# Gating of the second attention moved a stage later, weight sums on GpSimd, and three weight loads issued later

## The reference

```python
def _merge(a_att, b_att, a_z, b_z, g_a, g_b, w_o_a, w_o_b, w_out):
    o_a = (a_att * jax.nn.silu(a_z)) @ w_o_a
    o_b = (b_att * jax.nn.silu(b_z)) @ w_o_b
    merged = jax.nn.sigmoid(g_a) * o_a + jax.nn.sigmoid(g_b) * o_b
    return merged @ w_out
```

```python
    kv = x @ kv_w                       # keys and values
    q = (x @ w_q).reshape(...)          # queries
```

## Time and profile before

| | us |
|---|---|
| median of 3 runs (lowest, highest) | 3465.53 (3465.18, 3466.58) |
| the profiled execution | 3466.58 |
| its span | 3464.7 |
| matrix engine busy in the span | 3048.4 (88%) |
| VectorE busy | 1214.3 (35%) |
| ScalarE busy | 844.5 (24%) |
| GpSimd busy | 413.3 (12%) |

### The profile page before, as it was taken

One profiled execution on the slowest core, in us unless ns is written; L12 is line 12 of the kernel. 1 busy time (PEld: TensorE's weight loads), 2 busy tenths in 40 slices (PEclk: granted clock), 3 DMA queues, 4 the chain that ended last, 5 costly groups with the idle time before them and its releaser, 6 DMA issues. The chain is left out here.

```text
span 3464.7 us, 41966 instructions
## 1 busy us (share of the span) xinstructions
PE 3048.4 (88%) x16815; PEld 1726.1 (50%) x16815; DVE 1214.3 (35%) x2312; ACT 844.5 (24%) x1772; POOL 413.3 (12%) x398
## 2 busy tenths in 40 slices
PE   8998999887777699888777749999999989999999
PEld 4446975322222567533222226555655536656785
DVE  2435633300000426640000042365632234376533
ACT  1411243000000214410000033345421113345310
POOL 0014510200000000220000011200001111210021
PEclk9999989998988799999988879999999999999999
DMA  6431514899997725279999942121021023121221
GB/s 215 170 137 64 214 50 160 332 427 406 412 407 328 267 98 171 62 297 426 404 424 391 415 162 49 47 48 50 1 73 49 25 85 92 48 48 50 74 73 61
DMA packets 174516, 633.20 MB, mean 183 GB/s; under 512 B 70222, under 2 KB 72684, under 8 KB 148336
## 3 DMA queue, kind: packets, MB, share of 16 engines
q1 hardware_dynamic: 147696, 475.65, 36.4%
q10 hardware_dynamic: 8064, 114.30, 7.9%
q0 software_dynamic: 18560, 40.50, 3.3%
HBM read 590.71 MB, written 67.05 MB: 190 GB/s over the span
## 5 line engine op out<-in xcount | busy, mean ns | idle before, releaser
L1637 PE MATMUL banks<-weight_ring,experts_xT 128*32 128x512 f32 (+1 forms) x2240 | 359.0, 603 | 25.7 <-DMA weight_ring<-in_moe_w 15.7
L1655 PE MATMUL banks<-weight_ring,experts_hT 128*32 128x512 f32 (+1 forms) x1216 | 259.9, 658 | 133.2 <-DMA weight_ring<-in_moe_w 131.3
L1637 PEld LDWEIGHTS banks<-weight_ring,experts_xT 128*32 128x32 f32 (+1 forms) x2240 | 106.9, 118 | 224.0 <-issue 216.0
L1655 PE MATMUL banks<-cols,experts_hT 128*32 128x512 f32 (+1 forms) x448 | 178.5, 673 | 40.2 <-DMA cols<-in_moe_w 40.2
L1655 PEld LDWEIGHTS banks<-weight_ring,experts_hT 128*32 128x32 f32 (+1 forms) x1216 | 73.0, 127 | 259.5 <-DMA weight_ring<-in_moe_w 145.5
L2925 ACT ACTIVATE rows<-banks,pairs_low 128x768 f32<-128x768 f32 (+1 forms) x160 | 130.4, 815 | 184.9 <-DVE pairs_low L2980 90.9
L718 PE MATMUL banks<-cols,weight_ring 128*128 128x512 f32 x384 | 170.0, 598 | 1.0 <-PEq L302 1.0
L1637 PE MATMUL banks<-cols,experts_xT 128*32 128x512 f32 (+1 forms) x640 | 169.3, 593 | 0.3 <-DMA experts_slot<-in_moe_w 0.3
L2898 PE MATMUL banks<-token_cols,weight_ring 128*128 128x512 f32 (+1 forms) x384 | 169.1, 550 | 0.1
L1699 DVE COPY experts_y<-banks 128x512 f32<-128x512 f32 x32 | 22.1, 692 | 389.4 <-PE banks L1655 389.4
L1637 PE MATMUL banks<-experts_slot,experts_xT 128*32 128x512 f32 (+1 forms) x448 | 155.1, 593 | 1.2 <-issue 1.2
(11 more groups left out here) (536 smaller groups left out, 5372.3 us busy)
## 6 DMA issues: line engine op xcount, KB each, us to landing
weight_ring<-in_moe_w SPq DMA_DIRECT2D x96, 2048.0 KB, 22.7
weight_ring<-in_moe_w ACTq DMA_DIRECT2D x36, 2048.0 KB, 15.9
cols<-in_moe_w SPq DMA_DIRECT2D x22, 2048.0 KB, 24.0
experts_slot<-in_moe_w SPq DMA_DIRECT2D x20, 2048.0 KB, 23.8
cols<-in_moe_w ACTq DMA_DIRECT2D x18, 2048.0 KB, 16.0
weight_ring<-in_w_in SPq DMA_DIRECT2D x16, 2048.0 KB, 7.9
weight_ring<-in_w_ada SPq DMA_DIRECT2D x12, 2048.0 KB, 12.9
weight_ring<-in_a_w_in SPq DMA_DIRECT2D x8, 2048.0 KB, 11.4
```

The source lines that it names most:

```text
L1637: mm = pe.matmul(bank[a:a + n, :], self.xT[:, 4 * part + k, a:a + n], slots(r, part)[:, k, c:c + 512], start=part == k == 0, stop=part == ...
L1655: mm = pe.matmul(self.out[c][a:a + n, :], self.hT[:, f, a:a + n], slots(r, 2)[:, f, c * 512:c * 512 + 512], start=f == 0, stop=f == 3)
```

## The change

Four edits:

1. `diff_cols` is called with `ahead=3`: SP issues no weight load in it, only the store of the rows. The three loads are issued at the start of the product stage. There VectorE makes T1 and T2 of the first quad first, and waits for the stored rows behind them.
2. The gating of B leaves the pairs stage: its Silus and products stand at the start of the gate stage, on the same engines. S4 and S3 stand behind them, since they are written over z of B.
3. All weight sums of the gate stage are made by GpSimd, in a list with its gating (of quad q-1, between T4 of quad q and T1 of quad q+1) and its additions.
4. The matrix engine waits for a token sum by itself where it used to be covered by the wait for a weight sum (`summed`).

```diff
-    stage_to_cols(K, "diff_cols", K.H, K.HT, NT, first=K.keep_rows)
+    stage_to_cols(K, "diff_cols", K.H, K.HT, NT, first=K.keep_rows, ahead=3)
...
                     if i == nw:
-                        silus(0)
-                silus(1)
+                        silus()
...
                     if i == nw + 4:
-                        times(0, nw - 1)
-                times(1, N - 1)
+                        times(nw - 1)
...
+    def summed(self, pe, q, s):
+        tag = self.quads[q].tag
+        if (s, tag) not in self.seen:
+            self.seen.add((s, tag))
+            pe.wait_ge(*self.V.at(s + tag))
+
     def pe_p5(self, pe, q):
-        pe.wait_ge(*self.V.at(f"T1_{self.maker(q)}"))
+        pe.wait_ge(*self.W.at(f"T1_{self.maker(q)}"))
         if q >= 2:
             pe.wait_ge(*self.V.at(f"c12_{q - 2}"))
+        self.summed(pe, q, "S1")
         self.product(pe, q, 5, 2, True, False)
...
+            for c in range(4):
+                z = ZB[:, c, 0:2 * nb * P]
+                act.activation(z, z, ACT.Silu).then_inc(*S(f"z{c}"))
             for i in range(0, len(oa), 2):
                 act.wait_ge(*E.at(f"oa{i}"))
...
+            def sums(q):
+                F.make_t1(pool, q)
+                F.make_t2(pool, q)
+                F.make_t3(pool, q)
+            sums(0)
+            for q in qq:
+                F.make_t4(pool, q)
+                if 1 <= q <= NA:
+                    gated(q - 1)
+                if q + 1 < N:
+                    sums(q + 1)
+                if q in late:
+                    a = NO * late.index(q)
+                    for i in range(a, a + NO):
+                        pool.wait_ge(*V.at(f"ob{i}"))
+                        if i == 0:
+                            pool.wait_ge(*G.at(f"m{NA - 1}_3"))
+                        pool.tensor_tensor(merged(i), merged(i), gate_of(i), ALU.add).then_inc(*G(f"add{i}"))
...
         def _(dve):
-            for i in (1, 2, 3, 4):
-                tokens.make(dve, V, i)
-            F.dve_t1(dve, 0)
-            F.dve_t2(dve, 0)
-            F.dve_t3(dve, 0)
+            tokens.make(dve, V, 1)
+            tokens.make(dve, V, 2)
+            for c in range(4):
+                x = CB[:, c, 0:2 * nb * P]
+                dve.wait_ge(*S.at(f"z{c}"))
+                dve.tensor_tensor(x, x, ZB[:, c, 0:2 * nb * P], ALU.mult).then_inc(*V(f"zb{c}"))
+            dve.wait_ge(*V.at("zb3"))
+            tokens.make(dve, V, 4)
+            tokens.make(dve, V, 3)
...
         @block.vector
         def _(dve):
+            F.make_t1(dve, 0)
+            F.make_t2(dve, 0)
             dve.wait_ge(*K.rows_kept())
             tokens.make(dve, V, 1)
-            F.dve_t1(dve, 0)
             tokens.make(dve, V, 2)
-            F.dve_t2(dve, 0)
```

More of the change, by code:

```diff
@@ L2771, in stage_pairs @@
     filled, emptied = (Tally(K, f"pairs_{x}", range(len(flat))) for x in ("filled", "emptied"))
-    silu = Tally(K, "pairs_silu", [(g, j) for g in range(2) for j in range(4)])
+    silu = Tally(K, "pairs_silu", range(4))
     for i, u in enumerate(flat):
@@ L2947, in empty, with silus @@
                         emptied_upto[0] += 1
-                def silus(g):
-                    for j, (_, _, z) in enumerate(gated[g]):
-                        act.wait_ge(*emptied.at((na if g == 0 else len(flat)) - 1))
-                        act.activation(z, z, ACT.Silu).then_inc(*silu.up((g, j)))
+                def silus():
+                    for j, (_, _, z) in enumerate(gated):
+                        act.wait_ge(*emptied.at(na - 1))
+                        act.activation(z, z, ACT.Silu).then_inc(*silu.up(j))
                 for i in range(N + 1):
@@ L3006, in outs, with times @@
                         dve.tensor_copy(q_of(i), out_bank).then_inc(*out.up(i))
-                def times(g, i):
-                    if i is not None:
-                        dve.wait_ge(*out.at(i))
-                    for j, (y, x, z) in enumerate(gated[g]):
-                        dve.wait_ge(*silu.at((g, j)))
+                def times(i):
+                    dve.wait_ge(*out.at(i))
+                    for j, (y, x, z) in enumerate(gated):
+                        dve.wait_ge(*silu.at(j))
                         dve.tensor_tensor(y, x, z, ALU.mult).then_inc(K.gated, 1)
-                        K.n_gated += 1
                 for i in range(N + 2):
@@ L3222, with __init__ @@
 class Quads:
-    def __init__(self, K, n0, quads, E, S, V, emptied=None):
+    def __init__(self, K, n0, quads, E, S, V, W=None, emptied=None):
         self.K, self.n0, self.quads = K, n0, quads
         self.E, self.S, self.V = E, S, V
+        self.W = W or V
         self.emptied = emptied or (lambda q: S.at(f"e21_{q}"))
@@ L3283, in pe_p6 @@
         pe.wait_ge(*self.S.at(f"s1_{q}"))
-        pe.wait_ge(*self.V.at(f"T2_{self.maker(q)}"))
+        pe.wait_ge(*self.W.at(f"T2_{self.maker(q)}"))
+        self.summed(pe, q, "S2")
         self.product(pe, q, 6, 0, False, False)
@@ L3288, in pe_p3 @@
         pe.wait_ge(*self.S.at(f"p5_{q}"))
-        pe.wait_ge(*self.V.at(f"S4{self.quads[q].tag}"))
+        self.summed(pe, q, "S4")
         self.product(pe, q, 3, 2, False, True)
@@ L3641, in stage_merge @@
     pe_l = [f"oa{i}" for i in range(len(oa))]
-    act_l = [f"oa{i}" for i in range(0, len(oa), 2)]
-    dve_l = ["S1", "S2", "S3", "S4", "T1_0", "T2_0", "T3_0"] + [f"oa{i}" for i in range(1, len(oa), 2)]
+    act_l = [f"z{c}" for c in range(4)] + [f"oa{i}" for i in range(0, len(oa), 2)]
+    dve_l = ["S1", "S2"] + [f"zb{c}" for c in range(4)] + ["S4", "S3"] + [f"oa{i}" for i in range(1, len(oa), 2)]
     late = (N - 3, N - 1)
+    pool_l = ["T1_0", "T2_0", "T3_0"]
     for q in qq:
@@ L3649, in stage_merge @@
         ahead = q + 1 < N
-        dve_l += [f"T4_{q}", f"c11_{q}"] + [f"T1_{q + 1}", f"T2_{q + 1}"] * ahead + [f"c12_{q}"] + [f"T3_{q + 1}"] * ahead + [f"c22_{q}"]
+        dve_l += [f"c11_{q}", f"c12_{q}", f"c22_{q}"]
+        pool_l += [f"T4_{q}"] + [f"m{q - 1}_{i}" for i in range(4)] * (1 <= q <= NA) + [f"T{i}_{q + 1}" for i in (1, 2, 3)] * ahead
         if q in late:
@@ L3655, in stage_merge @@
             dve_l += [f"ob{i}" for i in range(a, a + NO)]
-    pool_l = [f"m{q}_{i}" for q in range(NA) for i in range(4)] + [f"add{i}" for i in range(len(ob))]
+            pool_l += [f"add{i}" for i in range(a, a + NO)]
     E, S, V, G = K.steps("quads", pe=pe_l, act=act_l, dve=dve_l, pool=pool_l)
-    F = Quads(K, n0, quads, E, S, V)
+    F = Quads(K, n0, quads, E, S, V, W=G)
     K.w.free[n0 + WA] = E.at(f"oa{len(oa) - 1}")
@@ L3765, in _, with gated @@
         def _(pool):
-            for q in range(NA):
+            def gated(q):
                 for i in (0, 1, 2, 3):
@@ L4189, in second_layer @@
     stage_pairs(K, f"pairs{l}", units, nw, (z_units(0, ZA), z_units(2, ZB)), window_bias,
-                ([(CA[:, c, 0:nt * P], QA[:, c, 0:nt * P], ZA[:, c, 0:nt * P]) for c in range(4)],
-                 [(CB[:, c, 0:nt * P], QB[:, c, 0:nt * P], ZB[:, c, 0:nt * P]) for c in range(4)]))
+                [(CA[:, c, 0:nt * P], QA[:, c, 0:nt * P], ZA[:, c, 0:nt * P]) for c in range(4)])
     M1 = B.lower.rearrange("p (c n) -> p c n", n=TA)
```

86 lines of the change are left out of this document (38 added, 48 removed).

## The result

| kernel | median us | lowest to highest | executions |
|---|---|---|---|
| before | 3465.36 | 3462.06 to 3466.58 | 4 |
| changed | 3445.44 | 3438.92 to 3448.03 | 4 |

The ratio is 0.9944, with a 95% interval of 0.9927 to 0.9962: a small gain (0.6%) that is clear of 1, 19.9 us where 12.5 were forecast. The profiled execution of the changed kernel took 3445.88 us, with a span of 3444.0 (before: 3464.7).

A forecast was written before the change was run, and what follows sets the result against it. The matrix engine bounds the gate stages, leaving only stage edges to gain. Terms of 4.0 + 6.0 + 2.5 = 12.5 us took the median from 3465.53 to 3453.0 us, range 3449.5 to 3458.5.

The forecast's parts named there:

- all three edges: Start of the differential products, and the passage from pairs stage to gate stage in layers 0 and 1.
- layer 1's 2.5 us: Pairs-to-gate edge of layer 1: the gate stage starts at 3253.7 instead of 3256.26, gaining 2.5 us.
- the clock does not fall here now: Old pairs-to-gate edge of layer 1: no clock fall in the kernel before, so no clock gain added to 2.5 us.
- Edge one, 4.0 us: In front of the differential products: product 5 starts 6.3 us earlier, less 2.3 us for a fallen clock.
- its bound of 6.3: Upper bound in front of the differential products: 6.3 us gained if the clock holds.
- The rival "the clock holds": In the 3.9 us gap before product 5 the clock stays up: 2.3 us more gained, 3450.7; chance 0.17.
- Layer 0, 6.0 us: Pairs-to-gate edge of layer 0: 4.4 us from the earlier start, 1.6 us from the clock; 6.0 taken.
- GpSimd and VectorE in the gate stage, 0 us: Gate stages: added VectorE work and GpSimd's weight sums cost nothing, with 2.8 us of GpSimd cover in layer 1.
- The prediction's rival on VectorE: Start of gate stage: GpSimd delays VectorE, free at 13.4 us against 15.7; dearer hand-overs lose 2 us, 3455; chance 0.06.
- a GpSimd that becomes the bound: Middle quads of layer 1's gate stage: doubled GpSimd times cost 15.6 us, giving 3468.6; chance 0.06.
- a clock that falls in layer 0: Pairs-to-gate edge of layer 0: the clock falls all the same, 1.6 us less gained, 3454.6; chance 0.12.
- edges held by something else: At the edges: an instruction fetch or another engine's end holds them, half the gain lost, 3459; chance 0.07.

The follow-up runs named there:

- the run with four additions: The changed kernel with four more 128 x 512 additions on GpSimd in each middle quad of both gate stages, into an unused buffer: 3451.95 us.
- sums_on_dve: The changed kernel with the gate stages' weight sums T1 to T4 given back to VectorE, the gating staying in the gate stage: 3445.25 us, ratio 0.9942.
- before_again: The kernel before, unchanged, measured and profiled once more: 3467.32 us, ratio 1.0005.
- diff_only: The kernel before with only the differential's edits (`ahead=3`, T1 and T2 ahead of the wait for the stored rows): 3457.37 us, ratio 0.9978.
- busy4: The changed kernel with four matmuls whose result nobody reads, between the first products of quad 0 and product 5: 3444.96 us, ratio 0.9942.
- store_first: The changed kernel with two of the three weight loads moved behind the store of the rows: 3442.01 us, ratio 0.9934.
- store_in_two: The changed kernel with two loads moved behind the rows' store, and that store issued as first quarter and remaining three quarters: 3437.25 us, ratio 0.9921.

## Why the prediction was right, and where it was wrong

The mechanism came as forecast at all three edges; the sum of 12.5 us was too small and the range too narrow. What failed are sizes: layer 1's 2.5 us, with "the clock does not fall here now" (3.7 measured); the stretch behind layer 0, which the sum put at nothing (1.4 measured); and "about 0.2%, 6.9 us, is what a measurement of this kernel can tell", on which the range gave no room for the executions' own spread.

**Edge one, 4.0 us: right.** Products 0.32 us after the copy, product 5 held by S1 and the store, the clock lost behind the gap. Over the profiles the old form has a mean of 172.7, the new (seven profiles without a further edit there) 168.0: 4.6 us, between the forecast and its bound of 6.3, because the clock held in two of the seven. The rival "the clock holds", given 0.17, thus comes true in some executions. These two have the shortest gaps of the seven (3.52 and 3.59 us; the others 3.63 to 4.24), so the gap's exact length may decide as much as chance; but behind the 3.2 us of layer 1's old edge the clock fell in two profiles and held in one.

**Layer 0, 6.0 us: right** (234.7 to 228.6 = 6.1).

**Layer 1, 2.5 us: mis-sized.** It gave 157.2 − 153.5 = 3.7 us on average. The step that failed is "the clock does not fall here now": read from one execution, and not so in two of three, where the old edge cost 1.6 to 1.7 us more.

**GpSimd and VectorE in the gate stage, 0 us: right**, with the cover at 3.0 us against 2.8 by the run with four additions, and GpSimd's sums at a median of 1.29 us. The prediction's rival on VectorE had its mechanism right: GpSimd's first sums did hold VectorE up, which reached its first copy 13.6 us into the stage against the 13.4 of that rival and the 10.6 at most of the forecast, and this stayed covered, as both say. (The 1.11 us operation by which the rival was sized is an addition of GpSimd, L3779, not a gating.) A time lost to VectorE, a GpSimd that becomes the bound, a clock that falls in layer 0 or edges held by something else show in none of the profiles of the changed kernel. The Trainium skill's *SBUF — State Buffer*, section "SBUF: two separate sides", has VectorE and GpSimd exclude each other; S1 at 2.88 us beside GpSimd and 1.76 without it agrees, and the 1.1 us are nearly the length of the one GpSimd sum that began with it (1.28). The Trainium skill's advice in *GPSIMD Engine Reference*, section "Performance versus the Vector engine", to leave elementwise work on VectorE would have cost nothing here: sums_on_dve is as fast.

**The range and the spread: wrong.** The terms, averaged over profiles, give 4.6 + 6.1 + 3.7 = 14.4 us for the program's gain, and 17.3 ± 2.4 were measured. Some 1.4 us of the rest lie in the stretch between the layers (mean 272.2 with the old edge of layer 0, 270.8 with the new one), where the granted clock of the first 10 us was 0.83 in each of the three old profiles and in one of the ten new ones (the changed kernel's first, 272.1 us), and 1.00 in the other nine. The prediction has no term for it. What starts that fall is open, and the last 1.5 us are not told apart from noise. The larger mistake is the statement that 0.2%, 6.9 us, is what a measurement can tell, and a range of 9 us on top of it. I took the 1.4 us between three executions for the spread of the kernel. It is 25 us between the ends of 69. Medians of four differ by a few us by themselves: of the 19.9 us first measured, 17.3 ± 2.4 are the program's and the rest, some 2.6, is luck in the four executions on each side. With a standard deviation of 4.4 us the median of four executions is uncertain by 4 to 5 us to either side; the result lies 4.1 us under the range, and one widened by that much would just have held it.

## What to carry to other kernels

Where the matrix engine is busy inside a stage, look for time at its edges, and follow what is next in line there: moving SP's issues uncovered a store, and issuing it ahead of two loads and in two parts, by what its reader overwrites, then took some 5 us from the stretch (168.0 on average to 162.8 in the one profile), at least as much as the move itself had gained (4.6). Before sizing a few us from one profile, take a second profile of the same kernel and compare stretch by stretch: what differs between the two is luck and belongs into the range, and a clock that holds behind a short gap in one need not hold in the next. Work moved from VectorE to GpSimd is free only by its cover per quad, and it slows the two-input VectorE operations that run beside it.

## What the runs showed of the hardware

- The granted clock fell to 0.50 in the recurrence in nine of 13 profiles, at 459 to 461, 486 to 488 or 527 us, for 6.8 to 23.9 us, and not at all in four. The code up to there is the same in all, and the changed kernel alone has falls at 459, 487 and 486. Ahead of the falls at 459.4 (before) and 487.7 (before_again) the matrix engine had paused for 0.94 and 1.24 us, up to 456.5 and 484.9; from there on, and all the time that the clock was low, it was busy without a break, on tiles of 64 columns or 64 rows. In diff_only it paused for 0.92 us between 483 and 486 and no fall followed. The recurrence took 83.1 to 90.7 us with a fall and 79.9 to 81.2 without.
- After a gap of 3.5 to 4.2 us in front of product 5 the clock fell in five of seven profiles; after 1.7 us or less there, in none of three (busy4, store_first, store_in_two). In front of layer 1's gate stage it fell with a gap of 3.2 us in two of three and with 0.65 us in none of ten.
- A two-input VectorE operation of 1.76 us took 2.88 beside two-input GpSimd operations, and a GpSimd sum of 1.3 us took 2.7 beside it.
- A store of 2 MB took 8.9 us to land after 6 us in which the DMA had moved nothing, and 10.6 to 11.3 behind two more loads; as a quarter and three quarters, 4.6 and 7.8 (store_in_two).
